# A kernel of two transformer blocks with a mixture of experts: the experts' down weights are loaded from ScalarE's DMA queue

## The reference

```python
def swiglu(h, w_gate, w_up, w_down):
    return (jax.nn.silu(h @ w_gate) * (h @ w_up)) @ w_down

def moe_swiglu(h, w_router, w_gate, w_up, w_down):
    """Top-2-of-8 routed SwiGLU (softmax over the selected logits)."""
    logits = (h @ w_router).astype(jnp.float32)
    top_val, top_idx = lax.top_k(logits, TOP_K)
    ...
    for e in range(N_EXPERTS):
        y = swiglu(h, w_gate[e], w_up[e], w_down[e])
        out = out + gates[..., e:e + 1].astype(h.dtype) * y
```

## Time and profile before

| | |
|---|---|
| median of 3 runs | 1715.86 us (1714.61 to 1716.14) |
| profiled execution, device time | 1716.64 us |
| its span, first to last instruction | 1714.9 us |
| TensorE busy | 1686.8 us (98%), mean granted clock 0.995 |
| VectorE busy | 1374.2 us (80%) |
| ScalarE busy | 1118.0 us (65%) |
| DMA, SyncE's queue q1 | 476.43 MB, 74.5% of 16 engines' span |
| DMA, ScalarE's queue q10 | 1.84 MB, 0.3% |
| experts' part | from about 450 to 1345 us |

### The profile page before, as it was taken

How to read it: one execution, slowest core, us unless ns; L and a number is a source line. 1 busy time by engine, 2 the same in 40 slices (tenths; PEclk the granted TensorE clock), 3 DMA queues, 4 the chain that set the end, 5 groups by cost and what they waited for, 6 DMA issues and landing times.

```text
span 1714.9 us, 24639 instructions
## 1 busy us (share of the span) xinstructions
PE 1686.8 (98%) x9514; PEld 1461.7 (85%) x9514; DVE 1374.2 (80%) x1099; ACT 1118.0 (65%) x911; POOL 145.2 (8%) x152
## 2 busy tenths in 40 slices
PE   9999999999989999999999999999999899999999
PEld 8879999898878888888888888888888798889998
DVE  7576454746889998999998999989999789778775
ACT  6445343464557888777887788777877655855553
POOL 7200000000010200000000000000000018500000
PEclk9999999999999999999999999999999999999999
DMA  7455655553479999999999999999999654326551
GB/s 255 169 149 193 201 173 195 172 178 143 163 294 390 411 408 406 362 384 414 402 408 367 378 407 408 403 363 394 395 410 403 241 167 134 113 99 221 176 194 50
DMA packets 181300, 479.76 MB, mean 280 GB/s; under 512 B 11807, under 2 KB 80185, under 8 KB 166857
## 3 DMA queue, kind: packets, MB, share of 16 engines
q1 hardware_dynamic: 180185, 476.43, 74.5%
q10 hardware_dynamic: 1008, 1.84, 0.3%
HBM read 477.18 MB, written 1.05 MB: 279 GB/s over the span
## 4 chain that ended last, share of the span: by engine, by line
PE 74%; DVE 10%; issue 5%; ACT 4%; DMA 4%; POOL 2%; DVEq 0%; ACTq 0%; SPq 0%; POOLq 0%
PE bank L2251 19%; PE bank L2253 19%; PE bank L2252 19%; DVE wl L1729 6%; DMA arena<-in_moe_w_down 3%; ACT wh L1150 2%; PE bank L2257 2%; PE bank L2258 2%; PE bank L2781 1%; PE bank L2370 1%; PE bank L2378 1%; PE bank L2371 1%; POOL arena L925 1%; POOL arena L924 1%; DMA raw<-in_moe_w_down 1%
## 5 line engine op out<-in xcount | busy, mean ns | idle before, releaser
L1729 DVE TENSOR_TENSOR wl<-raw,wh 128x2048 fp32r<-128x2048 f32 x224 | 508.8, 2299 | 54.1 <-ACT wh L1150 53.3
L1150 ACT ACTIVATE wh<-raw 128x2048 fp32r<-128x2048 f32 x224 | 426.8, 1918 | 108.7 <-PE bank L2253 80.4
L2251 PE MATMUL bank<-wh,xhl 128*128 128x512 f32 x768 | 303.5, 395 | 4.5 <-issue 4.5
L452 DVE TENSOR_TENSOR wl<-raw,wh 128x2048 fp32r<-128x2048 f32 x112 | 254.8, 2292 | 64.8 <-ACT wh L445 63.0
L2253 PE MATMUL bank<-wh,xhl 128*128 128x512 f32 x768 | 299.9, 391 | 0.0
L2252 PE MATMUL bank<-wl,xhl 128*128 128x512 f32 x768 | 299.7, 390 | 0.0
L2251 PE MATMUL bank<-xhl,wh 128*128 128x256 f32 x944 | 268.0, 284 | 0.2 <-DVE wl L452 0.2
L2253 PE MATMUL bank<-xhl,wl 128*128 128x256 f32 x944 | 267.1, 283 | 0.0
L2252 PE MATMUL bank<-xhl,wh 128*128 128x256 f32 x944 | 267.1, 283 | 0.0
L1729 DVE TENSOR_TENSOR wl<-arena,wh 128x2048 fp32r<-128x2048 f32 x112 | 256.9, 2308 | 8.9 <-ACT wh L1150 8.1
L445 ACT ACTIVATE wh<-raw 128x2048 fp32r<-128x2048 f32 x116 | 219.3, 1912 | 33.1 <-PE bank L2253 19.5
(11 more groups left out here) (485 smaller groups left out, 2459.4 us busy)
## 6 DMA issues: line engine op xcount, KB each, us to landing
raw<-in_moe_w_up SPq DMA_DIRECT2D x96, 1024.0 KB, 7.9
raw<-in_moe_w_gate SPq DMA_DIRECT2D x64, 1024.0 KB, 7.8
raw<-in_moe_w_down SPq DMA_DIRECT2D x64, 1024.0 KB, 8.2
arena<-in_moe_w_gate SPq DMA_DIRECT2D x48, 1024.0 KB, 7.8
arena<-in_moe_w_down SPq DMA_DIRECT2D x48, 1024.0 KB, 8.1
raw<-in_w_up SPq DMA_DIRECT2D x22, 1024.0 KB, 5.3
arena<-in_moe_w_up SPq DMA_DIRECT2D x16, 1024.0 KB, 10.4
raw<-in_gla_w_in SPq DMA_DIRECT2D x12, 1024.0 KB, 7.2
```

Source lines behind the costliest of these rows:

```text
L452: V.tensor_tensor(wl[:, i % NW, :], raw[:, i % NR, :], wh[:, i % NW, :].bitcast(F32), ALU.subtract).then_inc(lo_of[i][0], 1)
L1150: V.activation(wh[:, s, :], src, ACT.Copy).then_inc(sg("hi_moe"), 1)
L1729: V.tensor_tensor(wl[:, s, :], moe_raw(c)[0], wh[:, s, :].bitcast(F32), ALU.subtract).then_inc(lo_moe, 1)
L2251: T.matmul(o, xh, yh, start=first, stop=False)
```

## The change

`load_expert` moves out of SyncE's program and takes the issuing engine as an argument. SyncE leaves the down pieces out; ScalarE loads them in its own `experts` body: at step c, behind the high part of piece c+4, it waits for the low part of piece c+2 and issues the load of piece c+8 if that is a down piece. For the experts' numbers each body of ScalarE begins with a wait for `more_ready` and two register loads, with the pair's number as a new argument. VectorE's body takes the argument and does not use it. Slots, sizes, semaphores and the condition for a load (the low part of the piece six before) stay.

```diff
@@ pairs
-            body(lambda a, b: b, True)
+            body(lambda a, b: b, True, 0)
...
-                body(lambda a, b: p * a + (a + b), True)
-            body(lambda a, b: more * a + ((NPAIR - 1) * a + b), False)
+                body(lambda a, b: p * a + (a + b), True, (p + 1) % NPAIR)
+            body(lambda a, b: more * a + ((NPAIR - 1) * a + b), False, NPAIR - 1)
@@ ahead of the engines' programs
+        def load_expert(eng, c, e):
...
+            eng.dma_start(to.rearrange("p (k n) -> p k n", k=src.shape[1]), src).then_inc(arrived, 16)
+
+        def by_act(c):
+
+            return porder[c][1] == "d"
@@ SyncE
                 for c in range(OWN, PC):
-                    moe_split(sp, lambda a, b: p * a + b, c - NRX)
-                    load_expert(c, e)
+                    if not by_act(c):
+                        moe_split(sp, lambda a, b: p * a + b, c - NRX)
+                        load_expert(sp, c, e)
...
             for c in range(OWN, PC + NR):
+                if c < PC and by_act(c):
+                    continue
                 moe_split(sp, lambda a, b: more * a + ((NPAIR - 1) * a + b), c - NRX)
@@ ScalarE
-            def experts(at, more_follow):
+            def experts(at, more_follow, pair):
...
+                act.wait_ge(sg("more_ready"), 2)
+                e = [act.value_load(order_i[0:1, bass.ds(2 * pair + i, 1)], min_val=0, max_val=NE - 1) for i in range(2)]
                 for c, (i, kind, j, k) in enumerate(porder):
...
                     if c + NW < PC or more_follow:
                         moe_hi(at, c + NW)
                     elif c < PC - 2:
                         hi.upto(N_PRE + c + NW - PC)
+                    if c + 8 < PC and by_act(c + 8):
+                        moe_split(act, at, c + 8 - NRX)
+                        load_expert(act, c + 8, e)
```

More of the change, by code:

```diff
@@ L659, in build @@
         head_pairs = [(("so", hp), (slice(None), slice(2 * hp, 2 * hp + 2), slice(None))) for hp in range(SH // 2)]
+        def load_expert(eng, c, e):
+            i, kind, j, k = porder[c]
+            ee = e[i]
+            to, arrived = moe_raw(c)
+            if kind == "d":
+                src = IN["moe_w_down"][0].rearrange("e f n -> (e f) n")[bass.ds(ee * FE + STEPS[j][0] + k * 256, 256), :]
+                src = src.rearrange("(p k) n -> p k n", p=P)
+            else:
+                f, width = STEPS[j]
+                n = PIECE // width * P
+                src = IN["moe_w_gate" if kind == "g" else "moe_w_up"][0, bass.ds(ee, 1), k * n:(k + 1) * n, f:f + width]
+                src = src.rearrange("a (k p) n -> p (a k) n", p=P)
+            eng.dma_start(to.rearrange("p (k n) -> p k n", k=src.shape[1]), src).then_inc(arrived, 16)
+        def by_act(c):
+            return porder[c][1] == "d"
         block = ctx.enter_context(nc.Block())
@@ L677, in load @@
                     n0 += n
[L679 to L692, removed]
             sp.wait_ge(sg("vrow_zero"), 1)
@@ L727, in _ @@
                 split_done(sp, N_PRE - NR + c)
-                load_expert(c, (0, 0))
+                load_expert(sp, c, (0, 0))
             for hp in range(SH // 2):
```

## The result

| | before | after |
|---|---|---|
| median | 1715.66 us (1714.61 to 1716.14, 4 runs) | 1740.53 us (1734.20 to 1743.69, 4 runs) |
| ratio, 95% interval | | 1.0144 (1.0129 to 1.0159) |
| profiled execution | 1716.64 us | 1734.2 us |
| mean granted clock in it | 0.995 | 0.993 |

The change costs 24.9 us. The forecast was +6.4 us, its range ended at 1732.

What follows compares the result with a forecast made beforehand. TensorE was taken to bound the kernel. Late up pieces cost 3.2 + 1.0 + 1.6 + 1.6 = 7.4 us, less 1.0 for earlier down pieces: +6.4, 1722.3 us on the median (1723.0 profiled), range 1713 to 1732.

Steps and rivals of the forecast that it cites:

- What bounds the kernel: Experts' part: TensorE, 99% busy, sets the end; earlier loads can give back at most its 11.7 us of low-part waits.
- SyncE's loss of issues gives nothing, ScalarE's issues cost nothing: 112 issues of 0.34 us leave an idle SyncE; on ScalarE they hide under splits: zero, 56 us if uncovered.
- The first body: Start of the first experts body: ScalarE's first split moves from 446.59 to 450.3, hidden from VectorE with 1.3 us left; zero.
- The start of ScalarE's load: A load on ScalarE's queue starts 3.5 us after its issue in a busy stretch, 1.0 on idle engines.
- Rival (c): ScalarE's queue starts as quickly as on idle engines, 1.0 us: price 17.4 us, time 1733.3; chance 0.07.
- From then on takes half of the bandwidth: Once started, ScalarE's load gets half the DMA bandwidth, so the up piece ahead is late by its remaining service time.
- The place: Last up piece, c = 79, of each pair pays: 3.2, 1.0, 1.6 and 1.6 us, sum 7.4.
- other groups have either more spare time or a shorter queue: Groups at c = 39, 63 and 75 were taken to add nothing to the sum.
- a pair pays its worst place once: Within a pair, a stall once paid is spare time for later pieces, so only its worst place counts.
- The side and the sizes: Whole kernel: chances of faster 0.10, same 0.38, slower 0.52; forecast +6.4 us.
- The gain of 1 us for earlier down pieces: First down piece of a group comes earlier, so some 1 us of TensorE's waits may go.
- GB/s unchanged: DMA engines' rate from 538 to 688 us, 407 GB/s, was taken as fixed.

Runs made afterwards that it cites:

- act_three: The changed kernel with only the down pieces of the groups at c = 16, 28 and 52 loaded by ScalarE, the rest by SyncE: 1718.37 us, ratio 1.0021.
- act_8k_again: The changed kernel run once more, unchanged, with down pieces in 8 KB packets on ScalarE's queue: 1741.13 us, ratio 1.0172 to the kernel before.
- act_72_2k: The changed kernel with only the group at c = 72 loaded by ScalarE and down pieces in 2 KB packets: 1741.19 us, ratio 1.0160.
- act_first: The changed kernel with ScalarE's wait and down-load issue put ahead of the split of piece c + 4 instead of behind it: 1744.53 us, ratio 1.0195.

## Why the prediction was wrong, and where it was right

**What bounds the kernel**: right. TensorE still sets the end, and the loss is its waits for low parts behind late up pieces. The 11.7 us counted some stands twice; 8.8 us is the better figure, which makes a gain smaller yet.

**SyncE's loss of issues gives nothing, ScalarE's issues cost nothing**: right. An issue took 0.34 us, and 48 of them with all waits and register loads cost no more than the 3.7 us of act_three. The count of ScalarE's busy time did not change.

**The first body**: right. ScalarE's first split there began later, 451.23 instead of 446.59 (450.3 was forecast), and VectorE came to it at 454.25, 0.8 us later than before. But VectorE was 0.8 us later already at the piece ahead, so nothing of it is the first body's.

```profile
451.23 3.72 ACT L1158 ACTIVATE wh<-arena 128x2048 fp32r<-128x2048 f32 x2 [5.08 <-PE bank L2760]
```

**The start of ScalarE's load**: right. 3.5 us was one sample; the eight groups c = 64 and 72 of after began 3.3 to 3.7 us behind the issue. Rival (c), the quick start of 1.0 us with 1733.3, has a number near the profiled 1734.2 and is wrong as a mechanism.

**"From then on takes half of the bandwidth"**: this step failed. The earlier trace rows show 144 packets of 0.52 MB beside 185 of 0.72: packets of about the same size, 3.6 and 3.9 KB. Equal counts and equal bytes can't be told apart in such a sample, and the prediction took the bytes. The Trainium skill ("DMA: Bandwidth & Descriptors", "Queues, rings and completion order") puts the turns in packets, and the prediction quoted it; by that rule one had to ask how long a packet is on each queue. The trace agrees that the turns go by count and not by bytes, with 105 against 105 and 127 against 124 packets; a packet of the profile is here one row of a partition, while the page's holds several descriptors, and how many of its rows the engine takes in one turn no run here shows. The 8 KB of a down packet could be read in the code, two neighbouring rows for each partition. The half share makes an up piece late by as much as it had left; the third share by up to twice, the fifth by up to four times as much, ending only when all down pieces issued so far have passed.

**The place**: failed too, and for a reason of its own. c = 79 was worked out because it had the least to spare, 0.65 us. But lateness is bounded by how much of the up piece is left and by how many bytes can pass it, so with an uneven share the spare time decides less than the packet size. c = 63 of the first pair had 1.02 + 0.26 = 1.3 us to spare, from the same traces; even by the half share (its last packets due at 609.2 + 9.7 - 0.5 = 618.4, q10's start at 615.1, so 3.3 us late) it should have had 3.3 - 1.3 = 2.0 us in the sum, and "other groups have either more spare time or a shorter queue" passed it over. c = 71, with 5.0 us to spare and 2 KB packets, was thought safe and paid in three pairs. c = 79 did not pay. Each pair had paid at 63 or 71 before, so "a pair pays its worst place once" may be why, but no run moved the group behind c = 79 alone. As a rule it held only for large stands (5 us at c = 63, then nothing at c = 71); behind 1.1 us at c = 63 the c = 71 of the same pair still lost 1.9 (act_8k_again).

**What was not in the sum**: the tail of a stand. The prediction ended the account of a late piece at TensorE's stand for it. The runs show that VectorE goes on being late behind it (1.0 us at c = 75 in two pairs), and that the long stands bring down the clock: 4 us at a mean of 0.62, 1.5 us more, in the first pair, and 3.3 us at 0.50, 1.7 us more, in the third. The prediction also costed what queues behind the new wait on ScalarE, not what the new issue is queued behind. That issue went out up to 7.1 us late, which cost nothing that these rows show with 8 KB packets; it did with 2 KB (4.7 to 5.3 us a pair in act_72_2k).

**The side and the sizes**: slower had the largest chance, 0.52, and the mechanism, a last up piece overtaken, was the one forecast. The term for it was 7.4 us; by the profiled execution it is 5.1 + 7.6 + 3.2 + 2.4 = 18.3 (c = 63, c = 71, c = 75 and 80, c = 39), less what comes back. The gain of 1 us for earlier down pieces is within that: ScalarE's waits for down weights went from 7.8 to 6.9 us. **GB/s unchanged**: 401 for 407 between 538 and 688 us, right but for the short holes.

**What stays open**: the median is 6.3 us above the profiled execution, and eight executions of this kernel go from 1734 to 1754 us, while those of before stay within 4 us. Part of it may be the clock: the trace of act_8k_again is of an execution 4.7 us longer than that of after, and TensorE worked at the lower level for 5.5 and 5.9 us of its two stretches instead of 3.2 and 3.4, which is 2.4 us of the 4.7. Its fourth pair paid at another place, so small shifts seem to decide that. The two executions of 1754 and 1756 us (the kernel after, and act_first) have no trace.

## What to carry to other kernels

A stream of loads that is consumed in order, and is nearly as fast as it has to be, should stay on one queue: a second queue gives no bandwidth, it gives up the order. Where two queues must share the DMA engines, look at the packet size on each, since the one with the smaller packets gets the smaller share while both have work, and ask which piece of it is wanted first. And when a DMA issue moves to an engine that also computes, look at what that engine may be standing for just ahead of the issue, and whether the load still lands in time: here it did with 8 KB packets and did not with 2 KB.

## What the runs showed of the hardware that I had not expected

- Two queues with packets of 8 and 4 KB moved 105 and 105 packets in 3 us, with 8 and 2 KB 124 and 127, with 4 and 2 KB 197 and 202. The bytes went 2:1, 4:1 and 2:1. With 2 KB on both the counts were 355 and 224, not equal, and why is not shown.
- The first packet of ScalarE's queue moved 3.3 to 3.7 us after the issue in all eight groups c = 64 and 72 of after, while q1 was busy; the 1.0 us of the earlier trace rows was on idle engines.
- On one queue, 8 KB packets in the down loads against 4 KB were worth 2.3 us of 1716, against 2 KB 16.5 (422 GB/s with 8 KB and 388 with 2 KB, q1 alone in before), and issuing a load in 2 KB packets took the sequencer 0.61 us, not 0.34.
- Four loads a pair out of order, 16 of 336, cost 18.5 us, three quarters of what all 112 cost.
